# Long convolutions of a hybrid backbone: from two groups of 96 bins to groups of 128, the upper 64 bins with both parts in one group

## What is computed

```python
def fft_long_conv(u, h, bias):
    L = u.shape[1]
    uf = u.astype(jnp.float32)
    spec = jnp.fft.rfft(uf, n=2 * L, axis=1) * jnp.fft.rfft(h, n=2 * L, axis=0)[None]
    y = jnp.fft.irfft(spec, n=2 * L, axis=1)[:, L // 2:L // 2 + L]
    return (y + uf * bias.astype(jnp.float32)).astype(u.dtype)

def hyena(u, conv_w, conv_b, w1, b1, w2, b2, w3, freq, bias):
    u = short_conv(u, conv_w, conv_b)
    v, x1, x2 = jnp.split(u, 3, axis=-1)
    h = implicit_filters(L, w1, b1, w2, b2, w3, freq)
    z = x1 * fft_long_conv(v, h[0], bias[0])
    return x2 * fft_long_conv(z, h[1], bias[1])
```

## Time and profile before

| | us |
|---|---|
| runs | 2157.66, 2154.71, 2159.97 (median 2157.66) |
| profiled execution | 2155.91, of which 2154.3 are the span of the profile |

### The profile page before, as it was taken

How to read it: one execution, slowest core, us unless ns; L and a number is a source line. 1 busy time by engine, 2 the same in 40 slices (tenths; PEclk the granted TensorE clock), 3 DMA queues, 4 the chain that set the end, 5 groups by cost and what they waited for, 6 DMA issues and landing times. The chain is left out here.

```text
span 2154.3 us, 25501 instructions
## 1 busy us (share of the span) xinstructions
PE 2017.5 (94%) x10290; PEld 1613.7 (75%) x10290; DVE 1251.4 (58%) x1184; ACT 1003.7 (47%) x916; POOL 37.9 (2%) x67
## 2 busy tenths in 40 slices
PE   6999999999899999999997887999999999999996
PEld 2677776678688877777786786888888888888884
DVE  2435543334533332337544445889898898979894
ACT  3221133433443432225124334777677676767772
POOL 3000000000000000100000000000000000000000
PEclk9999999999999999999998897999999999999998
DMA  8451120024222227732221244899899888979991
GB/s 344 192 212 42 62 75 30 32 87 146 72 91 95 94 98 281 300 123 101 83 87 59 91 167 162 323 354 373 304 375 359 347 340 346 389 293 376 355 375 45
DMA packets 62695, 435.03 MB, mean 202 GB/s; under 512 B 6992, under 2 KB 8016, under 8 KB 13056
## 3 DMA queue, kind: packets, MB, share of 16 engines
q1 hardware_dynamic: 57248, 396.39, 48.4%
q0 software_dynamic: 5344, 37.17, 4.3%
HBM read 432.48 MB, written 1.05 MB: 201 GB/s over the span
## 5 line engine op out<-in xcount | busy, mean ns | idle before, releaser
L1176 DVE TENSOR_TENSOR expert_lo<-expert_raw,expert_hi 128x2048 fp32r<-128x2048 f32 x264 | 598.8, 2289 | 89.9 <-ACT expert_hi L730 89.9
L730 ACT ACTIVATE expert_hi<-expert_raw 128x2048 fp32r<-128x2048 f32 x264 | 504.4, 1917 | 124.9 <-PE psum L1714 71.0
L844 DVE TENSOR_TENSOR units_lo<-raw_units,units_hi 128x2048 fp32r<-128x2048 f32 x102 | 216.6, 2124 | 406.4 <-ACT units_hi L509 406.4
L509 ACT ACTIVATE units_hi<-raw_units 128x2048 fp32r<-128x2048 f32 x102 | 181.4, 1778 | 557.1 <-PE psum L1291 473.8
L1289 PE MATMUL psum<-h_hi,units_hi 128*128 128x512 f32 (+1 forms) x928 | 354.6, 382 | 36.8 <-DVE units_lo L844 23.4
L1290 PE MATMUL psum<-h_lo,units_hi 128*128 128x512 f32 (+1 forms) x928 | 339.1, 365 | 0.0
L1291 PE MATMUL psum<-h_hi,units_lo 128*128 128x512 f32 (+1 forms) x928 | 338.9, 365 | 0.0
L1712 PE MATMUL psum<-expert_hi,gathered_hi_lo 128*128 128x512 f32 (+1 forms) x768 | 292.1, 380 | 3.4 <-DVE expert_lo L1176 2.3
L1713 PE MATMUL psum<-expert_lo,gathered_hi_lo 128*128 128x512 f32 (+1 forms) x768 | 287.1, 374 | 0.0
L1714 PE MATMUL psum<-expert_hi,gathered_hi_lo 128*128 128x512 f32 (+1 forms) x768 | 287.0, 374 | 0.0
L1289 PEld LDWEIGHTS psum<-h_hi,units_hi 128*128 128x128 f32 x928 | 179.0, 193 | 93.1 <-issue 31.0
(11 more groups left out here) (242 smaller groups left out, 2637.0 us busy)
## 6 DMA issues: line engine op xcount, KB each, us to landing
expert_raw<-in_moe_w SPq DMA_DIRECT2D x264, 1024.0 KB, 6.3
raw_units<-in_w_in SPq DMA_DIRECT2D x40, 1024.0 KB, 4.8
mod_units<-in_w_mod POOLq DMA_DIRECT2D x24, 1024.0 KB, 9.5
raw_units<-in_ffn_w SPq DMA_DIRECT2D x22, 1024.0 KB, 4.8
raw_units<-in_ffn_w SPq DMA_DIRECT2D x16, 704.0 KB, 4.5
raw_units<-in_w_pab SPq DMA_DIRECT2D x16, 512.0 KB, 3.5
raw_units<-in_w_o SPq DMA_DIRECT2D x8, 1024.0 KB, 4.8
mod_units_a<-in_w_mod SPq DMA_DIRECT2D x5, 1024.0 KB, 4.8
```

What stands on the lines that cost most here:

```text
L509: A(WH[:, s, 0:n], raw[:, s, 0:n], ACT.Copy).then_inc(hi_done, 1)
L730: A(EH[:, SPLIT_AT[j], :], eraw[:, RAW_AT[j], :], ACT.Copy).then_inc(e_hi, 1)
L844: TT(WL[:, s, 0:n], raw[:, s, 0:n], WH[:, s, 0:n].bitcast(F32), ALU.subtract).then_inc(lo_done, 1)
L1176: TT(EL[:, s, :], eraw[:, RAW_AT[j], :], EH[:, s, :].bitcast(F32), ALU.subtract).then_inc(e_lo, 1)
```

## The change

The lower 128 bins become one group (real and imaginary matrices of 128 columns), and the upper 64 bins another, whose real and imaginary part share the 128 partitions. For the product the second group is needed in two arrangements, so the forward transform makes it twice: once as real over imaginary, once as imaginary over real. The products of the high bins are then two multiplications and one addition (F[:, 3] is the real part twice, F[:, 4] imaginary parts with opposite signs). Counts per item: forward 8 matmuls before and after; VectorE 12 operations before, 9 after, with the second wait for y_d in front of the last three; inverse 16 matmuls before, 12 after. In the filter spectra, group 3 is made by two matmuls per chunk with 64 columns each, into partitions 0 to 63 and 64 to 127, from the same matrix columns. The tables grow from 5 x 96 to 9 x 64 columns (filter) and from 4 x 96 to 4 x 128 (forward); the inverse one keeps its size. Some tiles move by 1 KB. Names of the diff: HALF = 64.

```diff
 BLK = 256
 NB = FF // BLK
 NFFT = 384
-BINS = 96
+BINS = 128
+HALF = 64
 EPS = 1e-6
 SCALE = HD ** -0.5
 NEG = -1e30
...
-        dfti = place("dft_inverse", 23, [BINS, 4, L])
+        dfti = place("dft_inverse", 24, [BINS, 3, L])
...
-        dftks = [place("dft_filter0", 79, [P, 2, 5 * BINS]), place("dft_filter1", 96, [P, 2, 5 * BINS])]
+        dftks = [place("dft_filter0", 79, [P, 2, 9 * HALF]), place("dft_filter1", 96, [P, 2, 9 * HALF])]
-        mslots = [place("mod0_units_a", 83, [P, 2048]), place("mod0_units_b", 91, [P, 2048]),
+        mslots = [place("mod0_units_a", 84, [P, 2048]), place("mod0_units_b", 92, [P, 2048]),
-        Y = place("product_spectrum", 59, [BINS, 4, HY_W])
+        Y = place("product_spectrum", 59, [BINS, 3, HY_W])
...
 
             def spectrum_out(l, q):
                 act.wait_ge(f_pe, 11 * l + 4 + q)
-                A(spec[:, q // 5, q % 5, :], PS[0:BINS, (q + 2 * l) % 8, :], ACT.Copy).then_inc(f_ac, 1)
+                A(spec[:, q // 5, q % 5, :], PS[:, (q + 2 * l) % 8, :], ACT.Copy).then_inc(f_ac, 1)
 
             def filter_arg(j):
                 act.wait_ge(f_pe, j + 1)
...
                         n = conv_items
                         units = QK_AT[l][n - 4 * l]
                         F = spec[:, o]
-                        for j in range(2):
-                            dve.wait_ge(y_d, 2 * n + j + 1)
-                            if n and j == 0:
-                                dve.wait_ge(y_i, n)
-                            are, aim = PS[0:BINS, 6 - 2 * j, :], PS[0:BINS, 7 - 2 * j, :]
-                            fre, fim, fren = F[:, j], F[:, 2 + j], (F[:, 4] if j == 0 else F[:, 1])
-                            TT(Y[:, j, :], are, fre, ALU.mult)
-                            TT(pt[:, 0, :], aim, fim, ALU.mult)
-                            TT(Y[:, 2 + j, :], are, fim, ALU.mult)
-                            link(TT(pt[:, 1, :], aim, fren, ALU.mult))
-                            TT(Y[:, j, :], Y[:, j, :], pt[:, 0, :], ALU.subtract)
-                            last = TT(Y[:, 2 + j, :], Y[:, 2 + j, :], pt[:, 1, :], ALU.add)
-                            link(last) if j == 0 else last.then_inc(y_y, 1)
+                        dve.wait_ge(y_d, 2 * n + 1)
+                        if n:
+                            dve.wait_ge(y_i, n)
+                        are, aim = PS[:, 6, :], PS[:, 7, :]
+                        TT(Y[:, 0, :], are, F[:, 0], ALU.mult)
+                        TT(pt[:, 0, :], aim, F[:, 1], ALU.mult)
+                        TT(Y[:, 1, :], are, F[:, 1], ALU.mult)
+                        link(TT(pt[:, 1, :], aim, F[:, 2], ALU.mult))
+                        TT(Y[:, 0, :], Y[:, 0, :], pt[:, 0, :], ALU.subtract)
+                        link(TT(Y[:, 1, :], Y[:, 1, :], pt[:, 1, :], ALU.add))
+                        dve.wait_ge(y_d, 2 * n + 2)
+                        TT(Y[:, 2, :], PS[:, 4, :], F[:, 3], ALU.mult)
+                        link(TT(pt[:, 0, :], PS[:, 5, :], F[:, 4], ALU.mult))
+                        TT(Y[:, 2, :], Y[:, 2, :], pt[:, 0, :], ALU.add).then_inc(y_y, 1)
                         if l:
                             lo(b["qkv"] + units[0] + 2, units[0] % 2)
                         dve.wait_ge(y_i, n + 1)
...
                         pe.wait_ge(f_ac, 10 * l + 5 + q - 8)
                     o, g = q // 5, q % 5
                     for c in range(2):
-                        last = MM(PS[0:BINS, bank, :], dftks[l][:, c, g * BINS:(g + 1) * BINS], tapss[l][:, o, c, :],
-                                  start=c == 0, stop=c == 1)
+                        if g == 3:
+                            for h in range(2):
+                                last = MM(PS[h * HALF:(h + 1) * HALF, bank, :], dftks[l][:, c, 6 * HALF:7 * HALF], tapss[l][:, o, c, :],
+                                          start=c == 0, stop=c == 1)
+                        else:
+                            f = 7 * HALF if g == 4 else g * BINS
+                            last = MM(PS[:, bank, :], dftks[l][:, c, f:f + BINS], tapss[l][:, o, c, :],
+                                      start=c == 0, stop=c == 1)
                     last.then_inc(f_pe, 1)
 
             pe.sem_inc(e_use, NEXT0)
...
                             pe.wait_ge(y_z, n)
                         for j in range(2):
                             for g in range(2):
-                                f = slice((2 * g + j) * BINS, (2 * g + j + 1) * BINS)
+                                f = slice((2 * j + g) * BINS, (2 * j + g + 1) * BINS)
                                 for c in range(2):
                                     last = MM(PS[0:BINS, 6 - 2 * j + g, :], dftf[:, c, f], VT[:, c, :], start=c == 0, stop=c == 1)
                             last.then_inc(y_d, 1)
                         qk_half(units[0], 1)
                         pe.wait_ge(y_y, n + 1)
                         for ch in range(4):
-                            for g in range(4):
+                            for g in range(3):
                                 last = MM(PS[:, 6 + ch // 2, (ch % 2) * L:(ch % 2 + 1) * L], Y[:, g, ch * P:(ch + 1) * P], dfti[:, g, :],
-                                          start=g == 0, stop=g == 3)
+                                          start=g == 0, stop=g == 2)
                         last.then_inc(y_i, 1)
                         for u in units[1:]:
                             for j in range(2):
...
     rates = np.abs(np.linspace(math.log(1e-2) / 1.5, math.log(1e-2) / 0.3, 2 * HY_W, dtype=np.float32))
     decay = np.exp(-dist[:, None] * rates[None, :]) + 0.05
 
+    nbins = NFFT // 2
     j = np.arange(L)[:, None].astype(np.float64)
-    k = np.arange(2 * BINS)[None, :]
+    k = np.arange(nbins)[None, :]
     w = 2 * np.pi / NFFT
     re, im = np.cos(w * j * k), -np.sin(w * j * k)
     nyq = np.cos(np.pi * j[:, 0])
...
     imn[:, 0] = nyq
     ren = re[:, :BINS].copy()
     ren[:, 0] = nyq
-
-    fwd = np.concatenate([re, imn], axis=1)
-    fil = np.concatenate([re, im * (k > 0), ren], axis=1)
+    low, high = slice(0, BINS), slice(BINS, nbins)
+
+    fwd = np.concatenate([re[:, low], imn[:, low], re[:, high], im[:, high], im[:, high], re[:, high]], axis=1)
+    fil = np.concatenate([re[:, low], (im * (k > 0))[:, low], ren, re[:, high], -im[:, high], im[:, high]], axis=1)
     n = (np.arange(L) + L // 2)[None, :]
-    kk = np.arange(2 * BINS)[:, None]
+    kk = np.arange(nbins)[:, None]
     ire = np.where(kk == 0, 1.0, 2 * np.cos(w * kk * n)) / NFFT
     iim = np.where(kk == 0, np.cos(np.pi * n), -2 * np.sin(w * kk * n)) / NFFT
-    inv = np.concatenate([ire, iim], axis=0).reshape(4, BINS, L)
+    inv = np.concatenate([ire[low], iim[low], ire[high], iim[high]], axis=0).reshape(3, BINS, L)
     c = np.arange(P) % GRID
     start = np.clip(c - WIN // 2, 0, GRID - WIN)[:, None]
     col = np.arange(GRID)[None, :]
...
```

## The result

The changed kernel took 2145.09 us (median of nine runs) against 2156.6 of the kernel before in the same session, a ratio of 0.9927 with an interval from 0.9908 to 0.9946. One of the nine took 3365.83 us at a mean clock of 0.555 and is left out of the ratio; without it the median is 2141.5. Over both, the mean of 15 runs is 2142.5 and that of the 105 runs of the kernel before that have their clock on record is 2157.6: 15.1 us less, with a standard error of 1.1. The forecast was 11.45 less. That 2145.09 lies so near the forecast 2146.2 is luck: it is the median with the run at 0.555 among the nine.

A forecast was written before the change was run, and what follows sets the result against it. PE was taken as the bound around the convolutions. Inverse -10.35, products' wait -1.6 and layer 1's spectra +0.5 sum to -11.45 us, from a median of 2157.66 to 2146.2 us; range 2141.2 to 2151.0.

The forecast's parts named there:

- inverse, six items: Inverse transform in both layers: 24 PE records per item instead of 32, 1.725 us less each, -10.35 us.
- wait for the products: Layer 1's first item: PE's 1.60 us wait for VectorE's last product goes with three operations fewer, -1.6 us.
- spectra of layer 1: Layer 1's filter spectra: two groups of 64-column halves add 2 x 0.3 less 0.1 us, +0.5 us.
- forward, transfers of the matrices: Forward transform with 128 output partitions keeps its pace, and loads of the larger matrices are covered: cost 0.
- pace of 0.2156 us for a record: Inverse transform on PE: each record keeps taking 0.2156 us, set by its 256 moving columns.
- no new wait inside an item: Convolution items: the second wait for the high bins costs nothing, and other waits keep their slack.
- d: Added time of one group 3 of the filter spectra, made as two 64-column halves: 0.3 us, possibly 0.3 to 2.0.
- Rivals 2 and 3: Group 3's halves: one after the other, d 2.0, chance 0.08; starts in program order, d 0.73, chance 0.12.
- rival 4: From layer 1's attention on, more pauses meet clock falls; measurably slower from about 32 us of such work, chance 0.03.
- Transfers ... Cost 0: Loads of the filter, forward and inverse matrices: 96 KB more take 4.8 us at most, under 8 us of cover.
- rival 1: Layer 0: the shorter pause after the spectra keeps the clock up, 3.0 us more gain, -14.45 in all, chance 0.22.
- the fall at 65 us: Clock at 0.50 after the pause behind layer 0's spectra, 3.0 us lost; the forecast counted it as staying.

The follow-up runs named there:

- e1: Kernel before with the inverse over three parts instead of four (imaginary part of the high half left out): 2146.51 us, ratio 0.9946.
- e2: Kernel before with 9 instead of 12 product operations per item, inverse matmul count unchanged: 2160.2 us, ratio 1.0002.
- e6: Kernel before with both cuts, inverse over three parts and nine product operations per item, filter spectra unchanged: 2143.43 us, ratio 0.9942.
- e3: Changed kernel with group 3's two 64-column halves issued one after the other instead of alternating by chunk: 2139.54 us, ratio 0.9909.

## Why the prediction came out as it did

| step | forecast | in the traces |
|---|---|---|
| inverse, six items | -10.35 | -7.06 in layer 0, -1.75 twice in layer 1: -10.56 |
| wait for the products | -1.6 | -3.47 less the 1.75 of the item: -1.72 |
| spectra of layer 1 | +0.5 | +0.52 at the projection's start, +0.35 behind it |
| forward, transfers of the matrices | 0 | 0 |
| code among layer 1's modulation loads | none | -1.2 to -1.3 |
| half clock in layer 1's attention | none | -0.7 to -1.1 |
| sum | -11.45 | -13.2 without, -14.1 with the last |

**Right.** The pace of 0.2156 us for a record, the contraction over 128 partitions at no cost, the forward transform at 7.03 us, the wait of the earlier trace rows that goes with three operations fewer, and no new wait inside an item. e1 and e2 show these effects one by one, e6 that they add up. The halves run side by side as argued from the earlier trace rows, with d = 0.37 against 0.3: the earlier trace rows had the right things in view (going in and coming out of the tile shape), 0.07 us too small. Rivals 2 and 3 (d = 2.0 and 0.73) are out, and so is rival 4: the half clock did not grow with the change. In layer 1's spectra the errors are small: d is larger than taken, 0.17 us of it go into the wait for the last copy (0.1 was forecast), and the waits for h_lo, which the prediction named without slack, take up 0.17 more.

**Wrong: "Transfers ... Cost 0".** This is the step that failed. It asked for the three matrices only. The change also takes 64 instructions out of TensorE's code in layer 0's items (8 records x 2 x 4) and puts 16 into its spectra, and code is a transfer too. The profile of before had what was needed: the queue of instructions on the page, and a 0.52 us wait for a modulation load in layer 1 that nothing in the rows of data explains. What the runs showed in its place is a term of -1.2 to -1.3 us, half of the gap between -11.45 and -13.8 at equal clock.

**Wrong: the clock as one fall that stays or goes.** The forecast spent its rival 1 on the fall at 65 us and gave it 3.0 us. The price was right (2.83 to 3.3), and in the first trace of the changed kernel the fall was indeed missing. But it isn't tied to the change: it is there or not in traces of either kernel (three of eight with the long pause, two of five with the short one). That rival 1's sum of -14.45 lies near the measured mean is luck. What does differ is small and elsewhere. Between 1105 and 1200 us all seven traces of the table with the shorter inverse have 17.1 us at half clock, all others 20.5 or 23.9. Why they have 3.4 us less there isn't settled: the work of that stretch is the same, only the moment at which it comes differs.

**Too narrow: the scatter.** The range's low end took 2 us for the scatter of a median. But a run's time moves by more, with how much half clock it has. Between 260 and 699 us (layer 0's attention and what follows) that was 13.7 to 30.7 us in four traces of the kernel before and 17.1 to 30.7 in three of the changed one. The first eight runs of the changed kernel fall in two groups, four up to 2137.92 and four from 2145.09 on, and their median lies between; further runs lie in between as well, and those of the kernel before form no such groups. 0.9927 and 0.9947 are two measurements of the same pair. The three runs that the forecast had, 2154.71 to 2159.97, lay all in the middle, and their spread of 5.3 us was read as the kernel's; over 105 runs it is 15.4 us (2149.22 to 2164.59).

What remains: at equal clock the traces explain 13.2 us, and the runs show 13.8 (15 runs) or 13.6 (21), with a standard error of 0.3. Whether the rest is more than scatter stays open.

## What to carry to other kernels

Count the instructions that a change adds or removes on TensorE, not only their time: they move every later packet of code, and one that fell among loads for which an engine waits cost 1.2 to 1.3 us here. When a stage that an edit doesn't touch gets faster or slower, compare its queues packet by packet before giving the time to the edit. And where a run's time goes with its mean clock, compare kernels at equal clock, or take many runs of each: here single runs scatter by some 4 us (standard deviation), so the difference of two means of a dozen runs is still uncertain by 1.6 us.

## What the hardware showed

A packet of TensorE's code (16 KB) holds one DMA engine for 1.0 us as a rule, up to 2.0. Four loads of 1 MB took 15.5 to 15.8 us with such a packet among them and 14.1 to 14.4 without.

Matmul records in different column halves of the array start in pairs 13 ns apart even when three records of the first half are queued ahead of the second's first (e3). Going to 64-column tiles and back costs 0.37 us, of which 0.14 lie in the group itself (1.86 us for what takes 1.72) and the rest around it.

VectorE's first product of an item takes 692 ns with 128 partitions and 687 with 96, the second 680 and 677.

The same program has 113 to 127 us at half clock from trace to trace (four traces of the kernel before, three of the changed one), and 103 to 134 in 105 runs by their mean clock; each us goes with 0.42 us of run time.
